# Prompt retention of a hybrid decoder layer: update and inner products as three passes of rounded parts

## The chip, the core and the metric

The kernel runs on one core of a Trainium2 chip. The metric is the device time of one execution in microseconds (us), lower is better. The engines are TensorE (PE for its matmuls, PEld for its weight loads), VectorE (DVE), ScalarE (ACT), GpSimd (POOL) and SyncE (SP), whose queue issues all the transfers here.

## The reference, cut to what matters

One decoder layer over 1024 prompt tokens and 64 sample tokens: projections, differential attention, retention, gated merge and a SwiGLU FFN, all in float32. The change touches the prompt's retention, which goes through 8 chunks of 128 tokens in each of 4 heads, with a state of 256x512:

```python
def ret_chunk(S, q, k, v, log_gamma):
    ...
    qk = jnp.einsum('bihd,bjhd->bhij', q, k) * decay[None]
    o = jnp.einsum('bhij,bjhe->bihe', qk, v)
    ...
    o = o + jnp.einsum('bihd,bhde->bihe', q * q_dec[None, :, :, None], S)
    ...
    S_new = jnp.exp(C * log_gamma)[None, :, None, None] * S + jnp.einsum('bjhd,bjhe->bhde', k * k_dec[None, :, :, None], v)
    return S_new, o
```

The sample tokens take one such step from a stored state; their part is computed in the same stretch of the kernel.

## The kernel before

The whole layer is one program for each engine, ordered by hand and tied by semaphores. Large matrix products run as three passes: weights and activations are held as a high part (rounded to fp32r) and a low part (the rest, rounded), and high x high, high x low and low x high are added up in PSUM. POOL makes both parts of each block of weights (`w_h`, L356, and `w_l`, L363).

The retention lies in a stage of its own. TensorE's row of work there is the gate projection: `ROWS = 32` rows of 24 slots, and a slot is three passes (L2046, `gate(n)` runs n slots). Between slots stand the pieces of 32 prompt chunks (`CHB`), one for every `BEAT = 21` slots, from slot `LAG = 96` on. Chunk c begins at slot `chunk_kg(c)`, called `at` below. At its start TensorE does `update(c, 0)` (L2079: half of the keys' contribution to the state) and `inner(c)` (L2085: masked scores times values), three slots later `rows_out` of the chunk before (L2101) and `across(c)` (L2092: queries times old state), at `at + 7` `update(c, 1)`, at `at + 10` the transposes of the next chunk's queries and keys (L2064), and at `at + 14` their product (L2071). All of these are fp32 matmuls. `sample_piece` puts the sample's work at fixed slots (L1968 to L2005).

The other engines keep in step through `Beside`: each walks its own list of slots up to a given one and then does a chunk's piece. ScalarE copies the transposes (L2201) and scales the keys by their decay (`k_dec`, L2209) at `at + 11`, and squares the output rows for their norm (L2220). DVE at `at + 4` multiplies the gate of the chunk before (L2351) and makes the new state's first half (L2343), at `at + 7` the norm (`dve_root`, Newton steps L2237 and L2239, then L2359), at `at + 9` the second half of the state, and at `at + 16` the masked score block of the next chunk (`between`, L2333). In rows 0 to 15 it also multiplies gates after each group of 8 slots (L2301). The sample's state updates on DVE are L2275. SP loads the next chunk's values (L1826) at `at + 10` and the queries and keys after that (L1820) at `at + 16`.

Buffers are views of large tiles: `acc` (here `acc1`, cut up by `fm_view`), `gain`, `edge` and `xs_flat`.

Of the kernel before, what the change touches and what calls it, by code (L numbers as in the profile page):

```python
# [34 lines left out]
D = 1024  # L35
# [157 lines left out]
def hybrid_layer(nc, x_prompt, x_sample, cache_k, cache_v, state_ret, page_table, norm_mix_g, w_in, b_gate,  # L193
# [54 lines left out]
    st.close()  # L248
    x_rows = acc1[:, :].rearrange("p (t d) -> p t d", d=D)
# [654 lines left out]
    def sp_vr_attention(sp):  # L904
# [68 lines left out]
        sp_load_inputs(sp, 0)  # L973
        store_half(2 * DH - 1)
# [708 lines left out]
    p_t = gain[:, 768:896]  # L1683
    np_t = gain[0:TS, 896:1024]
# [11 lines left out]
    k_dec = edge[:, 2944:3200]  # L1696
# [15 lines left out]
    kd_ready = sem("kd_ready")  # L1712
# [65 lines left out]
    def sp_load_inputs(sp, i):  # L1778

        sp.dma_start(n_decay, c_ret_new[i]).then_inc(n_loaded, 16)  # L1780
        sp.dma_start(n_qdec, c_ret_qdec[i]).then_inc(n_loaded, 16)
        sp.dma_start(nv_in, proj[TP:T, i * RV + VR:(i + 1) * RV + VR]).then_inc(n_loaded, 16)

    def sp_gates(sp):
# [47 lines left out]
        def load_own_keys(g):  # L1832

            if g == 0:
                sp.wait_ge(bank_full, G_FM)
            sp.wait_ge(own_ready, g + 1)
            for j in range(4):
                sp.dma_start(own_k[32 * j:32 * j + DS, :], own_rows(g, j, RK, KR)).then_inc(own_k_loaded, 16)
# [17 lines left out]
        def gate_steps():  # L1856

            for row in range(ROWS):
                g, r = divmod(row, 4)
                i = row // 8  # L1860
                for x in range(24):
# [7 lines left out]
                    if (r, x) == (1, 11) and g + 1 < 2 * RH:  # L1869
                        load_own_keys(g + 1)  # L1870
# [12 lines left out]
                    if (r, x) == (3, 1) and g + 1 < 2 * RH:  # L1883
                        load_own_values(g + 1)
# [73 lines left out]
    def pe_gates(pe):  # L1958
        def sample_piece(row, x):
# [30 lines left out]
            if (r, x) in UPDATES:  # L1990
# [6 lines left out]
                for q, bank in enumerate((BN, BA)):  # L1997
                    r0 = 32 * (2 * pair + q)
                    nc.tensor.matmul(psum[:, bank, :], own_k_dec[r0:r0 + DS, b * 128:(b + 1) * 128], own_v[r0:r0 + DS, :],  # L1999
                                     start=True, stop=True, tile_position=(r0, 0)).then_inc(nu_full, 1)  # L2000
# [132 lines left out]
    def act_gates(act):  # L2133
        def sample_piece(row, x):
# [3 lines left out]
            if (m, x) == (0, 14):  # L2138
                act.wait_ge(nt_full, i + 1)
                nc.scalar.copy(nqk_t, psum[:, BN, 0:2 * KT * TS].rearrange("p (k n) -> p k n", n=TS)).then_inc(nt_read, 1)  # L2140
            if (r, x) == (1, 2):
                act.wait_ge(own_k_loaded, 64 * (g + 1))
                act.wait_ge(rd_loaded[i % 2], 16 * (i // 2 + 1))
                act.wait_ge(nu_full, 8 * g)
                nc.scalar.activation(own_k_dec, own_k, ACT.Copy, scale=decay[i % 2][:, 132:133]).then_inc(own_ready, 1)
# [57 lines left out]
        def chunk_decay(c):  # L2203
# [5 lines left out]
            nc.scalar.activation(k_dec, rk_in, ACT.Copy, scale=decay[i % 2][:, 129:130]).then_inc(kd_ready, 1)  # L2209
# [3 lines left out]
        chunk_decay(0)  # L2213
        for c in range(CHB):
# [8 lines left out]
            if c + 1 < CHB:  # L2223
                chunk_t(c + 1)
                chunk_decay(c + 1)
        beside.to(math.inf)
# [17 lines left out]
    def dve_gates(dve):  # L2244
        def sample_piece(row, x):
# [14 lines left out]
            if (m, x) == (0, 20):  # L2260
                dve.wait_ge(nqk_full, i + 1)
                for h in range(2):
# [59 lines left out]
        dstep.done(nc.vector.memset(np_t, 0.0))  # L2322
# [4 lines left out]
        def between(c):  # L2327
# [5 lines left out]
            nc.vector.tensor_tensor(p_t, psum[:, BT, 0:128], decay[i % 2][:, 0:128], ALU.mult).then_inc(pt_ready, 1)  # L2333
# [27 lines left out]

        beside.to(LAG - 3)
        between(0)
        for c in range(CHB):
# [26 lines left out]
    tails = []  # L2391
    for kind, dt in (("f", F), ("r", R)):
        st = ExitStack()
        for half in ("high", "low"):
            sb(f"tail_{kind}_{half}", [128, KD * T], F, st)
        tails.append(sb(f"tail_{kind}", [128, KD * 128 + NT * D], dt, st))
        st.close()
    tail_f, tail_r = tails
# [791 lines left out]
```

## Time and profile before

| | us |
|---|---|
| median of 3 runs | 2775.54 |
| lowest, highest | 2775.37, 2775.61 |
| profiled execution, its own time | 2780.18 |
| its span | 2778.4 |
| TensorE matmuls busy | 2749.3 (99%) |
| DVE busy | 1280.8 (46%) |
| ScalarE busy | 720.0 (26%) |
| POOL busy | 862.8 (31%) |
| retention stage, chunks 0 to 31 | from 1068 to 1628 |

Times in rows of a timeline count from the first instruction of the profiled execution. Matmuls are pipelined and their busy times overlap, so what one costs is read from the distance of starts. A row of DVE that starts before the one ahead has ended is pipelined in the same way, by some 0.08 us.

### The profile page before, as it was taken

What the parts mean: (1) busy time and instruction counts of PE and PEld (TensorE: products, weight loads), DVE (VectorE), ACT (ScalarE), POOL (GpSimd) and SP (SyncE); (2) the same over time, 40 slices, a digit from 0 to 9 for tenths busy, and PEclk for the clock granted to TensorE, in tenths of its full rate; (3) what the DMA queues carried; (4) which work ended last, traced back from release to release, by engine and by line L of the source; (5) the groups of instructions that cost most, each with busy time, mean ns of one, the idle gap of its engine ahead of it and who ended that gap; (6) DMA issues with size and microseconds to landing.
All of it is one profiled execution on the core that took longest, in us unless ns stands there. A gap on an engine that the chain in (4) does not pass through costs nothing.

```text
span 2778.4 us, 41312 instructions
## 1 busy us (share of the span) xinstructions
PE 2749.3 (99%) x16146; PEld 2327.7 (84%) x16146; DVE 1280.8 (46%) x2468; ACT 720.0 (26%) x1518; POOL 862.8 (31%) x697
## 2 busy tenths in 40 slices
PE   8999999999999999999999999999999999999998
PEld 6888877777777778787777799999899999998886
DVE  6431355536555644454444432343375555543224
ACT  5111122225555532222111221011232222221011
POOL 2433422202211222221122233535023444455240
PEclk9999999999999999999999999999999999999999
DMA  4323356553333234456555454243122222245221
GB/s 149 119 92 133 106 197 205 201 168 123 97 121 126 82 126 165 156 186 193 183 168 180 154 196 139 103 148 137 66 89 70 71 79 86 71 148 173 84 60 64
DMA packets 277776, 362.11 MB, mean 130 GB/s; under 512 B 28514, under 2 KB 172514, under 8 KB 277602
## 3 DMA queue, kind: packets, MB, share of 16 engines
q1 hardware_dynamic: 277602, 359.74, 39.0%
q8 instruction: 116, 1.90, 0.3%
q14 instruction: 58, 0.48, 0.1%
HBM read 257.24 MB, written 111.35 MB: 133 GB/s over the span
## 4 chain that ended last, share of the span: by engine, by line
PE 95%; DVE 2%; ACT 1%; issue 1%; DMA 1%; SPq 0%; ACTq 0%; DVEq 0%
PE psum L530 22%; PE psum L1318 14%; PE psum L2677 14%; PE psum L2046 13%; PE psum L555 10%; PE psum L1011 3%; PE psum L1037 2%; PE psum L2659 2%; PE psum L2079 2%; PE psum L2092 2%; PE psum L1999 1%; PE psum L2701 1%; PE psum L1432 1%; PE psum L1027 1%; PE psum L2085 1%; PE psum L989 1%
## 5 line engine op out<-in xcount | busy, mean ns | idle before, releaser
L356 POOL TENSOR_TENSOR w_h<-stage,ones 128x512 fp32r<-128x512 f32 x268 | 303.8, 1161 | 1336.3 <-PE psum L2046 414.1
L363 POOL TENSOR_TENSOR w_l<-stage,w_h 128x512 fp32r<-128x512 f32 x268 | 355.8, 1355 | 123.4 <-DVE acc L1159 118.7
L530 PE MATMUL psum<-w_h,xt_h 128*128 128x512 f32 x864 | 344.4, 399 | 2.9 <-POOL w_l L377 2.0
L530 PE MATMUL psum<-w_h,xt_l 128*128 128x512 f32 x864 | 342.6, 396 | 0.0
L530 PE MATMUL psum<-w_l,xt_h 128*128 128x512 f32 x864 | 342.5, 396 | 0.0
L2046 PE MATMUL psum<-xt_h,w_h 128*128 128x384 f32 x744 | 288.8, 388 | 0.1
L2046 PE MATMUL psum<-xt_h,w_l 128*128 128x384 f32 x744 | 244.6, 329 | 0.0
L2046 PE MATMUL psum<-xt_l,w_h 128*128 128x384 f32 x744 | 244.6, 329 | 0.0
L408 POOL TENSOR_TENSOR w_l<-stage,w_h 128x512 fp32r<-128x512 f32 x106 | 139.3, 1314 | 268.8 <-ACT w_h L2771 268.7
L1318 PE MATMUL psum<-w_h,xt_h 128*128 128x512 f32 x512 | 218.1, 426 | 0.0
L1318 PE MATMUL psum<-w_l,xt_h 128*128 128x512 f32 x512 | 202.1, 395 | 0.0
L1318 PE MATMUL psum<-w_h,xt_l 128*128 128x512 f32 x512 | 201.7, 394 | 0.0
L530 PEld LDWEIGHTS psum<-w_h,xt_h 128*128 128x128 f32 x864 | 163.2, 189 | 44.4 <-issue 3.1
L530 PEld LDWEIGHTS psum<-w_l,xt_h 128*128 128x128 f32 x864 | 163.1, 189 | 39.4
L530 PEld LDWEIGHTS psum<-w_h,xt_l 128*128 128x128 f32 x864 | 163.2, 189 | 38.3
L2046 PEld LDWEIGHTS psum<-xt_h,w_h 128*128 128x128 f32 x744 | 140.6, 189 | 51.9 <-issue 50.5
L2677 PE MATMUL psum<-tail_r,w_h 128*128 128x272 f32 x648 | 172.2, 288 | 0.0
L2046 PEld LDWEIGHTS psum<-xt_l,w_h 128*128 128x128 f32 x744 | 140.7, 189 | 19.9 <-issue 19.9
L2907 DVE TENSOR_TENSOR acc<-acc,psum 128x512 f32<-128x512 f32 (+1 forms) x72 | 49.4, 687 | 209.3 <-PE psum L530 189.7
L2046 PEld LDWEIGHTS psum<-xt_h,w_l 128*128 128x128 f32 x744 | 140.1, 188 | 0.0
L555 PE MATMUL psum<-xt_h,w_h 128*128 128x384 f32 (+1 forms) x576 | 126.5, 328 | 0.0
L555 PE MATMUL psum<-xt_h,w_l 128*128 128x384 f32 (+1 forms) x576 | 126.5, 327 | 0.0
(300 smaller groups left out, 5584.3 us busy)
## 6 DMA issues: line engine op xcount, KB each, us to landing
stage<-in_w_in_dram SPq DMA_DIRECT2D x88, 512.0 KB, 5.7
proj<-edge SPq DMA_DIRECT2D x112, 256.0 KB, 2.0
out_dram<-acc SPq DMA_DIRECT2D x44, 512.0 KB, 3.5
stage<-in_w_gu_dram SPq DMA_DIRECT2D x88, 256.0 KB, 3.9
acc<-proj SPq DMA_DIRECT2D x82, 256.0 KB, 3.0
gates<-edge SPq DMA_DIRECT2D x32, 544.0 KB, 4.3
acc<-in_cache_k_dram SPq DMA_DIRECT2D x32, 512.0 KB, 5.7
acc<-in_cache_v_dram SPq DMA_DIRECT2D x32, 512.0 KB, 4.5
```

Of the source, the lines that this page charges most:

```text
L356: last = nc.gpsimd.tensor_tensor(w_h[s][:, a:b, :], src, one.unsqueeze(1).to_broadcast([128, b - a, WN]), ALU.mult)
L363: last = nc.gpsimd.tensor_tensor(w_l[s][:, a:b, :], stage[h][:, a - lo:b - lo, :], w_h[s][:, a:b, :].bitcast(F), ALU.subtract)
L408: nc.gpsimd.tensor_tensor(op_l(o), op_source(n, name), op_h(o).bitcast(F), ALU.subtract).then_inc(op_split, 1)
L530: last = nc.tensor.matmul(psum[:, bank, :], x, w[s][:, k, :], start=k == 0 and n == 0, stop=k == nk - 1 and n == len(passes) - 1)
L555: ins = nc.tensor.matmul(psum[:, g(3 * j + c)[1], 0:width], w[s][:, k, m * 128:(m + 1) * 128], x[:, k, a:a + width], start=k == 0 and n == ...
L1011: nc.tensor.matmul(psum[:, SB_ + 2 * c + a // 512, 0:width], q[r, qb % 4 * 128:(qb % 4 + 1) * 128], k_t[(2 * h + a // 512) % 3][r, 0:width ...
L1037: last = nc.tensor.matmul(psum[:, TB, 0:DV], mix_t[:, b * 128:(b + 1) * 128], v_in[(2 * h + b // 4) % 3][:, b % 4, :], start=b == 0, stop= ...
L1318: last = nc.tensor.matmul(psum[:, VB + u % 2, :], x, wt[s][:, k, :], start=k == 0 and n == 0, stop=k == KD - 1 and n == len(passes) - 1)
L2046: last = nc.tensor.matmul(psum[:, BG + q % 2, 0:width], wt[s][:, k, m * 128:(m + 1) * 128], x[:, k, a:a + width], start=k == 0 and n == 0, ...
L2079: nc.tensor.matmul(psum[:, BU, :], k_dec[:, k * 128:(k + 1) * 128], rv_in, start=True, stop=True).then_inc(upd_full, 1)
L2092: last = nc.tensor.matmul(psum[:, BO, :], qk_t[:, k, :], state[:, k, :], start=False, stop=k == KT - 1)
L2677: last = nc.tensor.matmul(psum[:, 2 * (no % 4) + c, 0:HC], w(o)[:, k, :], x_piece(x, k, low)[:, at], start=k == 0 and i == 0, stop=k == 3 ...
```

## The change

`update` and `inner` no longer multiply in fp32 but in three passes of fp32r parts. For that ScalarE writes the decayed keys rounded (`k_dec_high`) and, new at `at + 15`, the values rounded (`rv_high`). DVE writes the rest of the keys at `at + 13` (`k_dec_low`), makes the masked score block twice (`p_t` in fp32, `p_high` rounded) and subtracts (`p_low`), and at `at + 17` writes the rest of the values over the loaded ones (`rv_low`). One semaphore, `kv_split`, counts the four steps of a chunk; both updates wait for all four. The rounded parts lie in `tail_r`, an fp32r view of memory that `acc` and `xs_flat` cover.

To make room, the sample's values (`nv_in`) share `nr_rows` and load at slot 9 in place of 3 of a head's last row, its transposed queries and keys and its score block move into `gain`, with a memset for each head, and the own keys are scaled in place and loaded at slot 1 of a group's row 3 in place of slot 11 of row 1.

```diff
+    rv_in_at = fm_at[0]
     rv_in = fm_view(128, RV)
...
-    nv_in = fm_view(TS, RV)
     nr_rows = fm_view(128, RV)
+    nv_in = nr_rows[0:TS, :]
+    rv_at = fm_at[0]
+    fm_view(128, RV)
...
-    nqk_t = xs_flat[:, 0:256].rearrange("p (k n) -> p k n", n=TS)
+    p_high, p_low, p_t = tail_r[:, 0:128], tail_r[:, 128:256], xs_flat[:, 128:256]
+    rv_high, rv_low = (tail_r[:, KD * 128 + a:KD * 128 + a + RV] for a in (rv_at, rv_in_at))
     q_own = xs_flat[:, 256:512].rearrange("p (k b r) -> p k b r", k=KT, r=16)
-    own_k, own_k_dec = (xs_flat[:, 512 + RK * s:512 + RK * (s + 1)] for s in range(2))
+    k_dec_high, k_dec_low = (tail_r[:, 512 + RK * s:512 + RK * (s + 1)] for s in range(2))
...
         def load_chunk(c):
             if c >= 1:
                 sp.wait_ge(rt_full, c)
-                sp.wait_ge(kd_ready, c)
+                sp.wait_ge(kv_split, 4 * c - 2)
...
-                    if (r, x) == (1, 11) and g + 1 < 2 * RH:
-                        load_own_keys(g + 1)
...
                     if (r, x) == (3, 1) and g + 1 < 2 * RH:
+                        load_own_keys(g + 1)
                         load_own_values(g + 1)
...
+                    if row % 8 == 7 and x == 9 and i + 1 < RH:
+                        sp_load_own_rows(sp, i + 1)
...
         def update(c, k):
-            pe.wait_ge(kd_ready, c + 1)
-            pe.wait_ge(rv_loaded, 16 * (c + 1))
+            pe.wait_ge(kv_split, 4 * (c + 1))
             pe.wait_ge(state_ready, 2 * c + k)
-            nc.tensor.matmul(psum[:, BU, :], k_dec[:, k * 128:(k + 1) * 128], rv_in, start=True,
-                             stop=True).then_inc(upd_full, 1)
+            for n, (keys, values) in enumerate(((k_dec_high, rv_high), (k_dec_low, rv_high), (k_dec_high, rv_low))):
+                last = nc.tensor.matmul(psum[:, BU, :], keys[:, k * 128:(k + 1) * 128], values, start=n == 0, stop=n == 2)
+            last.then_inc(upd_full, 1)
 
         def inner(c):
             pe.wait_ge(pt_ready, c + 1)
             pe.wait_ge(rnorm_ready, c)
-            last = nc.tensor.matmul(psum[:, BO, :], p_t, rv_in, start=True, stop=c % NC == 0)
+            for n, (weights, values) in enumerate(((p_high, rv_high), (p_low, rv_high), (p_high, rv_low))):
+                last = nc.tensor.matmul(psum[:, BO, :], weights, values, start=n == 0, stop=c % NC == 0 and n == 2)
...
+        def values_high(c):
+
+            act.wait_ge(rv_loaded, 16 * (c + 1))
+            act.wait_ge(kv_split, 4 * c + 2)
+            nc.scalar.copy(rv_high, rv_in).then_inc(kv_split, 1)
...
+                dstep.done(nc.vector.memset(np_t, 0.0))
+                dstep.wait(dve)
...
-            nc.vector.tensor_tensor(p_t, psum[:, BT, 0:128], decay[i % 2][:, 0:128], ALU.mult).then_inc(pt_ready, 1)
+            dstep.done(nc.vector.tensor_tensor(p_t, psum[:, BT, 0:128], decay[i % 2][:, 0:128], ALU.mult))
+            dstep.done(nc.vector.tensor_tensor(p_high, psum[:, BT, 0:128], decay[i % 2][:, 0:128], ALU.mult))
+            dstep.wait(dve)
+            nc.vector.tensor_tensor(p_low, p_t, p_high.bitcast(F), ALU.subtract).then_inc(pt_ready, 1)
+
+        def keys_low(c):
+
+            i = c // NC
+            dve.wait_ge(kv_split, 4 * c + 1)
+            nc.vector.scalar_tensor_tensor(k_dec_low, rk_in, decay[i % 2][:, 129:130], k_dec_high.bitcast(F), ALU.mult,
+                                           ALU.subtract).then_inc(kv_split, 1)
+
+        def values_low(c):
+
+            dve.wait_ge(kv_split, 4 * c + 3)
+            nc.vector.tensor_tensor(rv_low, rv_in, rv_high.bitcast(F), ALU.subtract).then_inc(kv_split, 1)
...
-            beside.to(at + 16)
             if c + 1 < CHB:
+                beside.to(at + 13)
+                keys_low(c + 1)
+                beside.to(at + 16)
                 between(c + 1)
+                beside.to(at + 17)
+                values_low(c + 1)
```

DVE at the end of chunk 5, from the norm's last operation to the gate product behind the score block of chunk 6 (`waits` names the semaphores; lines are each kernel's own). Before:

```order
L2359 TENSOR_SCALAR acc<-psum,rope_diff,o_rstd 128x512 [waits dve_step]
L2301 TENSOR_TENSOR edge<-edge 128x384 [waits sg_ready]
L2255 TENSOR_TENSOR xs_flat<-xs_flat,gain 128x4x8 [waits nr_full,n_loaded,nt_read]
L2255 TENSOR_TENSOR xs_flat<-xs_flat,gain 128x4x8 x3
L2343 SCALAR_TENSOR_TENSOR acc<-acc,rope_diff,psum 128x512 [waits ro_full,upd_full]
L2263 TENSOR_TENSOR gain<-psum,edge 64x4x8 [waits nqk_full]
L2263 TENSOR_TENSOR gain<-psum,edge 64x4x8
L2301 TENSOR_TENSOR edge<-edge 128x320 [waits sg_ready]
L2333 TENSOR_TENSOR gain<-psum,rope_diff 128x128 [waits gate_mul,ro_full,qk_full,rd_loaded0]
L2301 TENSOR_TENSOR edge<-edge 128x384 [waits sg_ready]
```

The same place after the change, from the second half of the state on:

```order
L2392 SCALAR_TENSOR_TENSOR acc<-acc,rope_diff,psum 128x512 [waits ro_full,upd_full]
L2295 MEMSET gain 64x128 [waits nq_ready,nqk_full]
L2298 TENSOR_TENSOR gain<-psum,edge 64x4x8 [waits dve_step]
L2298 TENSOR_TENSOR gain<-psum,edge 64x4x8
L2376 SCALAR_TENSOR_TENSOR tail_r<-acc,rope_diff,tail_r 128x256 [waits kv_split]
L2336 TENSOR_TENSOR edge<-edge 128x320 [waits sg_ready]
L2367 TENSOR_TENSOR xs_flat<-psum,rope_diff 128x128 [waits gate_mul,ro_full,qk_full,rd_loaded0]
L2368 TENSOR_TENSOR tail_r<-psum,rope_diff 128x128
L2370 TENSOR_TENSOR tail_r<-xs_flat,tail_r 128x128 [waits dve_step]
L2382 TENSOR_TENSOR tail_r<-acc,tail_r 128x512 [waits kv_split]
L2336 TENSOR_TENSOR edge<-edge 128x384 [waits sg_ready]
```

The keys' low part (L2376) comes in ahead of the gate product, and three operations stand where the score block (L2333, now L2367) was the last: its second copy, its low part, and the values' low part (L2382).

TensorE at the start of chunk 6. Before:

```order
L2046 MATMUL psum<-xt_h,w_l 128x384
L2079 MATMUL psum<-acc,edge 128x512 [waits state_ready,rv_loaded,kd_ready]
L2085 MATMUL psum<-acc,gain 128x512 [waits rnorm_ready,pt_ready]
L2046 MATMUL psum<-xt_h,w_h 128x384
L2046 MATMUL psum<-xt_l,w_h 128x384
```

After:

```order
L2065 MATMUL psum<-xt_h,w_l 128x384
L2098 MATMUL psum<-tail_r 128x512 [waits state_ready,kv_split]
L2098 MATMUL psum<-tail_r 128x512 x2
L2105 MATMUL psum<-tail_r 128x512 [waits rnorm_ready,pt_ready]
L2105 MATMUL psum<-tail_r 128x512 x2
L2065 MATMUL psum<-xt_h,w_h 128x384
L2065 MATMUL psum<-xt_l,w_h 128x384
```

Two fp32 matmuls become six passes at the same place; the update's wait is now for `kv_split`, whose last step is DVE's L2382.

## Rows read from the trace of the kernel before

**Rows 1.** The page: busy time of TensorE, and the granted clock in 40 slices.
```profile
PE 2749.3 (99%) x16146; PEld 2327.7 (84%) x16146; DVE 1280.8 (46%) x2468; ACT 720.0 (26%) x1518; POOL 862.8 (31%) x697
...
PEclk9999999999999999999999999999999999999999
```

**Rows 2.** Waits, 1060 to 1628 us: total, times, longest.
```profile
POOL w_h L356 <- PE psum L2046: 414.1, 7, 64.4
...
PE psum L1999 <- DVE acc L2275: 0.9, 1, 0.9
```

**Rows 3.** Groups of instructions, 1060 to 1628 us: count, busy us, mean ns.
```profile
L2079 PE MATMUL psum<-acc,edge 128*128 128x512 f32 x128 | 65.3, 592 | 0.0
...
L2085 PE MATMUL psum<-acc,gain 128*128 128x512 f32 x64 | 32.7, 592 | 0.0
```

**Rows 4.** Timeline of TensorE, start of chunk 15: start, us, line.
```profile
1330.82 1.02 PE L2079 MATMUL psum<-acc,edge 128*128 128x512 f32 x2
1331.68 1.02 PE L2085 MATMUL psum<-acc,gain 128*128 128x512 f32 x2
...
1332.72 0.34 PE L2046 MATMUL psum<-xt_l,w_h 128*128 128x384 f32 x1
```

**Rows 5.** Timeline of TensorE in an earlier projection, 26 passes, first and last.
```profile
300.04 0.40 PE L530 MATMUL psum<-w_h,xt_h 128*128 128x512 f32 x1
...
305.88 0.39 PE L530 MATMUL psum<-w_h,xt_l 128*128 128x512 f32 x1
```

**Rows 6.** Single lines: duration in ns, min/median/max; the last is a group.
```profile
L2301 DVE TENSOR_TENSOR edge<-edge x48: 474/558/1326, 1018.4 to 1311.5; 128x384 f32<-128x384 f32 x32, 128x320 f32<-128x320 f32 x16
...
L2524 DVE TENSOR_TENSOR xt_l<-acc,xt_h x8: 1285/1294/2249, 1621.9 to 1643.2; 128x1088 fp32r<-128x1088 f32 x8
...
L2343 DVE SCALAR_TENSOR_TENSOR acc<-acc,rope_diff,psum x56: 736/744/750, 1087.5 to 1629.9; 128x512 f32<-128x512 f32 x56
...
L2201 ACT COPY acc<-psum 128x512 f32<-128x512 f32 x32 | 18.8, 587 | 67.1 <-PE psum L2064 66.8 <-ACT edge L2165 0.3
```

**Rows 7.** Timeline, DVE's score block and TensorE's update: chunks 1, 5, 6, 10, 24.
```profile
1080.62 0.28 DVE L2333 TENSOR_TENSOR gain<-psum,rope_diff 128x128 f32<-128x128 f32 x1
...
1082.06 1.02 PE L2079 MATMUL psum<-acc,edge 128*128 128x512 f32 x2
...
1150.70 0.29 DVE L2333 TENSOR_TENSOR gain<-psum,rope_diff 128x128 f32<-128x128 f32 x1 [0.24 <-DVE edge L2301]
...
1153.92 1.02 PE L2079 MATMUL psum<-acc,edge 128*128 128x512 f32 x2
...
1171.08 1.02 PE L2079 MATMUL psum<-acc,edge 128*128 128x512 f32 x2
...
1171.34 0.29 DVE L2333 TENSOR_TENSOR gain<-psum,rope_diff 128x128 f32<-128x128 f32 x1 [0.24 <-DVE edge L2301]
...
1240.85 0.28 DVE L2333 TENSOR_TENSOR gain<-psum,rope_diff 128x128 f32<-128x128 f32 x1
...
1241.98 1.02 PE L2079 MATMUL psum<-acc,edge 128*128 128x512 f32 x2
...
1490.39 0.28 DVE L2333 TENSOR_TENSOR gain<-psum,rope_diff 128x128 f32<-128x128 f32 x1
...
1490.47 1.02 PE L2079 MATMUL psum<-acc,edge 128*128 128x512 f32 x2
```

**Rows 8.** A Newton step's durations, two rows of a timeline, and POOL's groups, 1060 to 1628.
```profile
L2239 DVE SCALAR_TENSOR_TENSOR o_rstd<-o_newton,o_rstd x108: 159/159/1218, 1071.6 to 1628.7; 128x1 f32<-128x1 f32 x108
...
1162.81 5.00 POOL L363 TENSOR_TENSOR w_l<-stage,w_h 128x512 fp32r<-128x512 f32 x4
...
1164.13 1.21 DVE L2239 SCALAR_TENSOR_TENSOR o_rstd<-o_newton,o_rstd 128x1 f32<-128x1 f32 x1
...
L363 POOL TENSOR_TENSOR w_l<-stage,w_h 128x512 fp32r<-128x512 f32 x56 | 70.8, 1295 | 1.1
...
L356 POOL TENSOR_TENSOR w_h<-stage,ones 128x512 fp32r<-128x512 f32 x56 | 58.5, 1076 | 414.1 <-PE psum L2046 414.1
```

**Rows 9.** The load of a chunk's values, L1826, from issue to landing.
```profile
DMA to landing us min/median/max: 2.6/2.8/6.2
```

More of the change, by code:

```diff
@@ L248, in hybrid_layer @@
     st.close()
+    tails = []
+    for kind, dt in (("f", F), ("r", R)):
+        st = ExitStack()
+        for half in ("high", "low"):
+            sb(f"tail_{kind}_{half}", [128, KD * T], F, st)
+        tails.append(sb(f"tail_{kind}", [128, KD * 128 + NT * D], dt, st))
+        st.close()
+    tail_f, tail_r = tails
     x_rows = acc1[:, :].rearrange("p (t d) -> p t d", d=D)
@@ L973, in sp_vr_attention @@
         sp_load_inputs(sp, 0)
+        sp_load_own_rows(sp, 0)
         store_half(2 * DH - 1)
@@ L1682, in hybrid_layer @@
     nr_gate = gain[:, 512:768].rearrange("p (b n) -> p b n", b=VT)
-    p_t = gain[:, 768:896]
-    np_t = gain[0:TS, 896:1024]
+    nqk_t = gain[:, 768:1024].rearrange("p (k n) -> p k n", n=TS)
+    np_t = gain[0:TS, 768:896]
     n_qdec = gain[:, 1024:1088]
@@ L1711, in hybrid_layer @@
     rt_read = sem("rt_read")
-    kd_ready = sem("kd_ready")
+    kv_split = sem("kv_split")
     qk_full = sem("qk_full")
@@ L1781, in sp_load_inputs, with sp_load_own_rows @@
         sp.dma_start(n_qdec, c_ret_qdec[i]).then_inc(n_loaded, 16)
+    def sp_load_own_rows(sp, i):
+        sp.wait_ge(nrr_full, i)
         sp.dma_start(nv_in, proj[TP:T, i * RV + VR:(i + 1) * RV + VR]).then_inc(n_loaded, 16)
@@ L1836, in load_own_keys @@
             sp.wait_ge(own_ready, g + 1)
+            sp.wait_ge(nu_full, 8 * g)
             for j in range(4):
@@ L1998, in sample_piece @@
                     r0 = 32 * (2 * pair + q)
-                    nc.tensor.matmul(psum[:, bank, :], own_k_dec[r0:r0 + DS, b * 128:(b + 1) * 128], own_v[r0:r0 + DS, :],
+                    nc.tensor.matmul(psum[:, bank, :], own_k[r0:r0 + DS, b * 128:(b + 1) * 128], own_v[r0:r0 + DS, :],
                                      start=True, stop=True, tile_position=(r0, 0)).then_inc(nu_full, 1)
@@ L2139, in sample_piece @@
                 act.wait_ge(nt_full, i + 1)
+                act.wait_ge(nr_full, 2 * i)
+                if i == 0:
+                    act.wait_ge(a_stored[1], 16 * DH)
                 nc.scalar.copy(nqk_t, psum[:, BN, 0:2 * KT * TS].rearrange("p (k n) -> p k n", n=TS)).then_inc(nt_read, 1)
@@ L2143, in sample_piece @@
                 act.wait_ge(rd_loaded[i % 2], 16 * (i // 2 + 1))
-                act.wait_ge(nu_full, 8 * g)
-                nc.scalar.activation(own_k_dec, own_k, ACT.Copy, scale=decay[i % 2][:, 132:133]).then_inc(own_ready, 1)
+                nc.scalar.activation(own_k, own_k, ACT.Copy, scale=decay[i % 2][:, 132:133]).then_inc(own_ready, 1)
             if (m, x) == (1, 9):
@@ L2208, in chunk_decay @@
             act.wait_ge(upd_full, 2 * c)
-            nc.scalar.activation(k_dec, rk_in, ACT.Copy, scale=decay[i % 2][:, 129:130]).then_inc(kd_ready, 1)
+            nc.scalar.activation(k_dec_high, rk_in, ACT.Copy, scale=decay[i % 2][:, 129:130]).then_inc(kv_split, 1)
+        def values_high(c):
+            act.wait_ge(rv_loaded, 16 * (c + 1))
+            act.wait_ge(kv_split, 4 * c + 2)
+            nc.scalar.copy(rv_high, rv_in).then_inc(kv_split, 1)
         beside.to(LAG - 7)
@@ L2213, in act_gates @@
         chunk_decay(0)
+        beside.to(LAG - 3)
+        values_high(0)
         for c in range(CHB):
@@ L2225, in act_gates @@
                 chunk_decay(c + 1)
+                beside.to(at + 15)
+                values_high(c + 1)
         beside.to(math.inf)
@@ L2261, in sample_piece @@
                 dve.wait_ge(nqk_full, i + 1)
+                dve.wait_ge(nq_ready, i + 1)
+                dstep.done(nc.vector.memset(np_t, 0.0))
+                dstep.wait(dve)
                 for h in range(2):
@@ L2321, in dve_gates @@
         dstep.done(nc.vector.memset(q_own, 0.0))
-        dstep.done(nc.vector.memset(np_t, 0.0))
         nc.vector.memset(own_k, 0.0).then_inc(own_ready, 1)
@@ L2360, in normalise @@
                                     ALU.mult).then_inc(rnorm_ready, 1)
+        beside.to(LAG - 5)
+        keys_low(0)
         beside.to(LAG - 3)
         between(0)
+        beside.to(LAG - 2)
+        values_low(0)
         for c in range(CHB):
@@ L2390, in hybrid_layer @@
     h_keep = nc.dram_tensor("h_keep", [T, D], F).ap()
[L2391 to L2398, printed above, removed]
     READ_BY = {"A11": "c11", "S2": "u2", "A12": "c11", "S3": "u3", "S1": "u4", "A22": "c21", "S4": "c12"}
```

2 lines of the change are left out of this document (1 added, 1 removed).

## The prediction

> **What bounds the kernel now.** I read the page first: TensorE is busy 99% of the span, at 2.4 GHz (nine tenths or more of full speed granted in every slice), and the profiled execution took 2780.2 us with a span of 2778.4, against a median of 2775.54 [rows 1]. The list of waits, cut to the retention stage (1060 to 1628 us), then shows whom TensorE waits for there: only DVE's sample update, 0.9 us of 568 [rows 2]. So whatever makes TensorE's row of work shorter moves the end one for one, unless another engine is now late. POOL and ScalarE wait for TensorE in that stage and not the other way round; POOL's split of the next weights waits 414 us for it.
>
> **What the change takes off TensorE.** An update or an inner product was one fp32 instruction in the program, and shows as two records of 128x512, busy 592 ns each but overlapping [rows 3]. The start times tell the real price: update and inner product of chunk 15 (chunks are counted from 0) start at 1330.82 and the second gate matmul behind them at 1332.72; one gate matmul's pitch of 0.176 lies between, so two products take 1.72 us, 0.86 each [rows 4]. A pass of rounded parts of the same shape is in the trace in the earlier projections: 25 starts from 300.04 to 305.88, 0.2336 us each [rows 5]. Three are 0.70. The gain is 0.159 us for a product; there are 32 chunks with two updates and one inner product, 96 products: **15.3 us**. Bounds: the passes are the same kind of instruction with the same shape, so 0.2336 is close; 0.225 and 0.245 would give 17.8 and 12.0 us. The weight loads of these passes hide as those of the projections do, whose pitch contains them. Transposes, products of queries and keys, and the part of the old state stay fp32 and cost what they did.
>
> **What it adds.** Each chunk gets one more ScalarE operation (the values rounded, 128x512; the nearest row is the copy at 0.587 us) and four more on DVE: low part of the keys (128x256), a second masked score block and its low part (128x128), low part of the values (128x512). Update(c, 0) now waits for the last of these, and inner(c) for the score parts. Behind the waiting update stand all gate matmuls on TensorE, so a wait there moves the end.
>
> Durations: two-input DVE operations from SBUF take 0.558 us at 384 columns and 1.29 at 1088 [rows 6], 1.04 ns for a column, so 0.69 at 512 and 0.29 at 128; the scalar-tensor-tensor at 256 is L2343's 0.744 less 256 columns, 0.48. Operations that don't depend on each other start some 0.08 before the one ahead ends. From the end of the old score block (L2333) to the first pass of the update it is then 0.21 (second block) + 0.32 (low part, which waits for it) + 0.61 (values) + 0.25 (semaphore and the weight load that a waiting matmul can't hide; 0.1 to 0.3) = 1.39 us. TensorE comes 0.16 sooner, since update(c-1, 1) is shorter: 1.55. Where DVE is behind and works without a pause, the keys' low part pushes too: **1.95 us**.
>
> The slack against this is the start of L2079 less the end of L2333. In 25 of the 32 chunks it is 2.1 to 5.5 us, more than is needed outside POOL's stretches but in chunk 9. The short ones and one long one [rows 7]: chunk 10 has 1241.98 - 1241.13 = 0.85, and DVE is behind, so it waits 1.95 - 0.85 = 1.1. In the same way chunk 1 has 1.16, but its values' low part also stands behind a gate product (0.48 more): 1.3; chunk 24 has -0.2: 2.1; chunk 6 has -0.55, with a pause of 0.24 that takes some up: 2.3. Chunks 0, 14 and 15 (slack 1.2, 0.9, 0.8) give 0.2, 0.35 and 1.1; chunk 9, again behind a gate product, 0.3. Sum: **8.8 us**.
>
> Chunks 6, 10 and 15 are short because DVE got there late, and the rows say why [rows 8]: while POOL splits weights (seven stretches of 18 to 19 us in the stage), the small Newton steps of DVE, which read two SBUF operands, take 0.96 to 1.32 us in place of 0.16 and 0.22, each until one POOL instruction (1.08 or 1.30) has ended; operations with a PSUM operand keep their time. Three of the four new DVE operations have two SBUF operands, and so have this price: a wait to the end of POOL's running instruction, 0 to 1.3 us, for each. The Trainium skill, SBUF — State Buffer, section "Who interferes with whom", says the same: a DVE instruction with two SBUF inputs and a GpSimd instruction that reads SBUF exclude each other for the whole instruction; this rule speaks against the change, for without it the sum of waits would end at 8.8. Laying the new operations between the rows of DVE and POOL, each held to the end of the POOL instruction in which it would start, adds 0.8 in chunk 1, 1.7 in chunk 5 (which had 2.9 of slack), 0.9 in chunk 10, 1.0 in chunk 14, 0.8 in chunk 19 and 0.5 in chunk 24: **5.7 us**, 4 to 9 with POOL's stretches moved by up to 4 us against the chunks. (Chunk 5 is the long one among the rows.)
>
> What costs nothing, with its cover: the rounding on ScalarE (value load issued 1 us after the update, landing in 2.8 us, 6.2 at most [rows 9]; the copy then ends 2.2 us or more before the next update, and ScalarE waits for TensorE around it; if a landing takes 6 us in each chunk, 2 us are lost); the own keys' load moved from row 1 to row 3 of a group, past the store and load of the states on SP's queue, with its 1.5 us of issue and still over 20 us ahead of its scaling; the sample rows' values loaded eight slots later, over 10 us ahead of their use; a memset of 64x128 for each head (0.15 us on DVE, four times, two of them in chunks that are short: 0.3); the chunk load on SP that waits for the keys' low part, a whole chunk ahead.
>
> **Sum.** -15.3 + 8.8 + 5.7 + 0.3 for the memsets = -0.5 us. On the profiled execution 2780.2 becomes 2779.7; on the median, which lies 4.6 below it, 2775.0. A measurement here can tell about 0.2%, 5.6 us, from no change, so this is no change.
>
> **Rivals.**
> - *The waits stay at 8.8*: the port between DVE and POOL costs the new operations little, because they slip in between POOL instructions. For it: the gate products at 384 columns that meet POOL's stretches mostly take under 0.7 and only at worst 1.33 [rows 6]. Then -15.3 + 8.8 + 0.3 = -6.2: 2769.3.
> - *Hardly a wait*: DVE's lateness in chunks 6, 15 and 24 is chance of this execution's phase, and shorter TensorE work moves POOL's stretches away from the Newton steps. Then some 3 us of waits, -12: 2763. Against it: the stretches are released by TensorE itself, in the same rows of the gates, so the phase repeats.
> - *Slower*: the new operations lose their turn against POOL more than once. The place is the end of chunks 1, 5, 10, 14, 19 and 24; one more POOL instruction (1.2 us) in each is +7.2, the sum +6.7, 2782.2. It decides from a second lost turn a chunk on. Chunk by chunk POOL's instructions follow each other without a gap, which speaks for it; the Newton steps, which each get in after one, against it.
> - *The passes aren't cheap*: a pass at 0.29 us or more would eat the whole gain, and at the fp32 record's 0.43 the change would cost 41 us. The rows of the projections leave this 2 in 100.
>
> **How the numbers follow.** The forecast, with its waits of 10 to 19 us, 2771 to 2780: 0.56. Waits near 8.8: 0.18. Hardly a wait: 0.11. Lost turns: 0.13. Dear passes: 0.02. Faster by over 0.2% (below 2770.0) takes the hardly-a-wait case and most of the 8.8 case: 0.27; slower (above 2781.1) most of the lost turns and the dear passes: 0.14; within it 0.59. The forecast's own range is 2771 to 2780; the range of 8 in 10 takes in 2769 and some of the lost turns: 2766 to 2781.5.
>
> **What would show it.** Right: three passes of update and inner product starting 0.234 apart; TensorE waiting for DVE's values' low part, 8 to 11 times in 32, 1 to 3 us at a time, 12 to 17 us in all, at the ends of chunks 1, 5, 6, 10, 14, 15, 19 and 24; the new two-input DVE operations at 0.3 to 0.7 us outside POOL's stretches and up to 1.3 longer in them. Wrong: waits on the ScalarE rounding or on the value load; waits spread over all chunks; a sum of waits under 5 us; passes at another pitch.

## The result, and the profile after

The changed kernel takes **2784.65 us** (median of 8 runs, 2781.2 to 2787.5); the kernel before, beside it, 2775.74 (8 runs). (Of all runs below, one of the kernel with fp32 products and waits and one of the kernel before beside it took some 13 ms; they are left out.) The ratio is 1.0029, interval 1.0019 to 1.0040: slower by 8 us, 5 to 11. The forecast was 2775.0, no change, in a range of 2766 to 2781.5. The measured time lies beyond the range, on the side that had 14 in 100.

The profiled execution took 2784.83 us with a span of 2782.6. From the page, busy time, and under it the waits of TensorE in the whole span (us in total, times, longest):

```profile
PE 2739.6 (98%) x16242; PEld 2346.9 (84%) x16242; DVE 1339.6 (48%) x2599; ACT 739.0 (27%) x1550; POOL 867.5 (31%) x697
```

```profile
PE psum L2098 <- DVE tail_r L2382: 13.1, 7, 3.9
...
PE psum L2018 <- DVE acc L2310: 1.7, 2, 1.1
```

TensorE is busy 10 us less than before [rows 1], DVE 59 us more. A wait that [rows 2] didn't have is now the largest of TensorE: seven updates (L2098) wait for the low part of the values (L2382), 13.1 us in all. So far this is the forecast. What it didn't have is in the granted clock, in stretches of 10 us of the changed kernel behind three of these waits, and behind the longest of the others (columns: length, TensorE busy with its count, granted clock, share and GB/s of DMA):

```profile
1083.50:1093.50 10.00, 9.61 (x40) 0.83 0.20 71
1175.50:1185.50 10.00, 9.75 (x37) 0.66 0.08 31
1250.00:1260.00 10.00, 9.75 (x42) 0.83 0.16 46
1322.50:1332.50 10.00, 9.78 (x49) 1.00 0.10 28
...
1498.50:1508.50 10.00, 9.75 (x54) 1.00 0.20 70
```

A mean of 0.83 over 10 us is 3.4 us at 1.2 GHz in place of 2.4, and 0.66 is 6.8 us. The half of it is lost: 1.7, 3.4 and 1.7 us, 6.8 us that the kernel before did not lose at these places. This is one profiled execution, but the others agree in their mean granted clock: 0.995 or 0.996 in all eight of the changed kernel, 0.998 or 0.999 in all 66 of the kernel before that ran beside the experiments. The difference of the means, 0.003, is some 8 us of such a span (an estimate; 0.001 is 2.8 us). In chunk 1 the six passes of update and inner product follow the wait (timeline of TensorE; in brackets the 3.88 us of idle time ahead). They take 2.5 us, up to the gate matmul at 1086.40; six at 0.234 are 1.4:

```profile
1083.89 1.44 PE L2098 MATMUL psum<-tail_r 128*128 128x512 f32 x3 [3.88 <-DVE tail_r L2382]
1085.12 1.48 PE L2105 MATMUL psum<-tail_r 128*128 128x512 f32 x3
...
1086.40 0.47 PE L2065 MATMUL psum<-xt_h,w_h 128*128 128x320 f32 x1
```

The account of the stage goes from the first to the last matmul of the gate projection. L2046 started first at 1008.4 and last at 1617.1 us before; its counterpart after is

```profile
L2065 PE MATMUL psum<-xt_h,w_h x744: 302/337/741, 1006.6 to 1622.2; 128*128 128x384 f32 x124, 128*128 128x320 f32 x62
```

That is 608.7 us before and 615.6 after, +6.9. The passes bring -15.3; TensorE's pauses grew by 13.2 (from 1.7 to 15.0 us, summed over the timelines) and, since a pause is counted from the modelled end of a matmul 0.34 long that the next could have followed after 0.18, by some 1.1 more (seven pauses more than before); the clock took 6.8. The sum is +5.8, and 1.1 is left over. (By whole executions the two profiled ones are 4.7 us apart, since that of before lay 4.4 us over its median; 1.7 of it is a fall of the clock at 28 us, ahead of the stage.)

### The profile page after: what moved, and what is told of

It is laid out like the page before. It is cut to its first block, busy times and chain, and to the rows that moved or that the text cites. A ratio compares the mean times of both kernels' runs of the same rounds, so it can differ in the third digit from the quotient of the medians.

```text
span 2782.6 us, 41714 instructions
## 1 busy us (share of the span) xinstructions
PE 2739.6 (98%) x16242; PEld 2346.9 (84%) x16242; DVE 1339.6 (48%) x2599; ACT 739.0 (27%) x1550; POOL 867.5 (31%) x697
## 4 chain that ended last, share of the span: by engine, by line
PE 93%; DVE 4%; ACT 1%; issue 1%; DMA 1%; SPq 0%; DVEq 0%; ACTq 0%
PE psum L538 22%; PE psum L1327 14%; PE psum L2726 14%; PE psum L2065 12%; PE psum L563 10%; PE psum L1020 3%; PE psum L1046 2%; PE psum L2708 2%; PE psum L2112 2%; PE psum L2098 2%; PE psum L2018 1%; PE psum L2750 1%; PE psum L1441 1%; PE psum L1036 1%; PE psum L2105 1%
## 5 line engine op out<-in xcount | busy, mean ns | idle before, releaser
L2065 PE MATMUL psum<-xt_h,w_h 128*128 128x384 f32 x744 | 266.0, 358 | 0.1
L563 PE MATMUL psum<-xt_l,w_h 128*128 128x384 f32 (+1 forms) x576 | 126.5, 327 | 0.0
```

The costliest lines, as they stand in the source:

```text
L563: ins = nc.tensor.matmul(psum[:, g(3 * j + c)[1], 0:width], w[s][:, k, m * 128:(m + 1) * 128], x[:, k, a:a + width], start=k == 0 and n == ...
L2065: last = nc.tensor.matmul(psum[:, BG + q % 2, 0:width], wt[s][:, k, m * 128:(m + 1) * 128], x[:, k, a:a + width], start=k == 0 and n == 0, ...
```

## The experiments

Twelve kernels ran, each beside the kernel before on the same chip. In each diff the lines are those of the changed kernel unless said otherwise.

### The passes alone

```diff
-            pe.wait_ge(kv_split, 4 * (c + 1))
+            pe.wait_ge(kv_split, 2 * (c + 1))
...
-            for n, (keys, values) in enumerate(((k_dec_high, rv_high), (k_dec_low, rv_high), (k_dec_high, rv_low))):
+            for n, (keys, values) in enumerate(((k_dec_high, rv_high), (k_dec_high, rv_high), (k_dec_high, rv_high))):
...
-                keys_low(c + 1)
-                values_low(c + 1)
```

> Three passes as in the change, but all of the high parts; the low parts of keys, scores and values are left out (three DVE operations and the second score block less a chunk), the moves of the sample's buffers stay. Theory (the passes bring 15.3 us, and what was lost is waits for DVE's values and TensorE's clock after them): no waits of the update, no fall of the clock in the stage but the one at its end, 2760 to 2761 us, ratio 0.9945. Rival (the passes cost more than 0.2336 us in this place, or the moved buffers cost): 2766 us or more, without waits.

The diff is cut: the inner product takes its high parts three times in the same way, and the second score block, its low part and ScalarE's wait for the keys' low part are gone too.

Measured: 2761.27 us, ratio 0.9939 (0.9924 to 0.9954). TensorE waits for none of the parts. The groups of the passes, with nothing idle before them:

```profile
L2098 PE MATMUL psum<-tail_r 128*128 128x512 f32 x192 | 54.8, 394 | 0.0
L2105 PE MATMUL psum<-tail_r 128*128 128x512 f32 x96 | 27.3, 393 | 0.0
```

By the ratio the gain is 16.9 us (13 to 21). In the trace the gate's first matmuls start from 1005.5 to 1599.2, 593.7 us in place of 608.7: 15.0 us less, with the same two short waits for the sample and the same fall of the clock at the stage's end as before. That is the forecast's 15.3, and the moved buffers of the sample cost nothing that shows. What the changed kernel loses comes with the low parts and the waits for them.

### The waits without the gain

```diff
-            for n, (keys, values) in enumerate(((k_dec_high, rv_high), (k_dec_low, rv_high), (k_dec_high, rv_low))):
-                last = nc.tensor.matmul(psum[:, BU, :], keys[:, k * 128:(k + 1) * 128], values, start=n == 0, stop=n == 2)
-            last.then_inc(upd_full, 1)
+            nc.tensor.matmul(psum[:, BU, :], k_dec_low.bitcast(F)[:, k * 128:(k + 1) * 128], rv_low.bitcast(F), start=True,
+                             stop=True).then_inc(upd_full, 1)
```

> The changed kernel with one fp32 product in the place of each three passes, on the low parts' tiles (the values come out other): all the splitting and its waits, without the gain. Theory (gain 15.3 us, waits 13, clock 7): the changed kernel's time plus 15 us, less up to 2 for waits that shorten since TensorE comes later: 2798 to 2801 us, ratio 1.008 to 1.009. Rival (the passes brought much less than 15 us): 2790 or less.

The inner product is changed in the same way.

Measured: 2795.01 us, ratio 1.0065 (1.0047 to 1.0084), 3 us under the expected range. The trace says why: waits of 11.9 us in place of 13.1, and only two falls of the clock of 3.4 us at the waits, in place of 13.6 us in three places, 3.4 us less lost. 15.3 less these two is 10.7. The fall at the stage's end is missing in this profile too, 1.7 us more, which makes 9.0; the two profiled executions are 8.7 us apart, the medians 10.4.

```profile
PE psum L2097 <- DVE tail_r L2380: 11.9, 6, 3.9
```

### Does the wait bring the clock down?

A ladder of waits in the kernel **before**, which has no fp32r product in the chunks:

```diff
+        AGAIN = {7: 18, 12: 22, 16: 24, 21: 29, 26: 32}
...
+            for _ in range(AGAIN.get(c, 0)):
+                dstep.done(nc.vector.tensor_tensor(p_t, psum[:, BT, 0:128], decay[i % 2][:, 0:128], ALU.mult))
+                dstep.wait(dve)
             nc.vector.tensor_tensor(p_t, psum[:, BT, 0:128], decay[i % 2][:, 0:128], ALU.mult).then_inc(pt_ready, 1)
```

> The kernel before, fp32 products; DVE repeats the masked score block 18, 22, 24, 29 and 32 times in chunks 7, 12, 16, 21 and 26, so that the inner product of each waits some 0.9, 2, 3, 4 and 5 us. Theory (a wait of about 2 us or more makes the granted clock fall from 2.4 to 1.2 GHz for 3.4 us or twice that just after it): no fall after the first, one at least after each of the last three, 1.7 us lost for each 3.4. Rival (the falls in the changed kernel came from its fp32r passes or from POOL's stretches, and only happened to stand behind waits): none here.

The waits came out as meant (timeline of TensorE, in brackets the idle time ahead):

```profile
1191.53 0.70 PE L2085 MATMUL psum<-acc,gain 128*128 128x512 f32 x1 [0.82 <-DVE gain L2338]
...
1282.29 1.12 PE L2085 MATMUL psum<-acc,gain 128*128 128x512 f32 x2 [1.95 <-DVE gain L2338]
...
1356.82 1.22 PE L2085 MATMUL psum<-acc,gain 128*128 128x512 f32 x1 [3.04 <-DVE gain L2338]
...
1451.17 1.76 PE L2085 MATMUL psum<-acc,gain 128*128 128x512 f32 x2 [4.05 <-DVE gain L2338]
...
1547.93 1.22 PE L2085 MATMUL psum<-acc,gain 128*128 128x512 f32 x1 [5.20 <-DVE gain L2338]
```

and the granted clock in the 10 us from each (the number behind the count in brackets):

```profile
1191.00:1201.00 10.00, 9.47 (x40) 1.00 0.68 239
1282.00:1292.00 10.00, 9.71 (x50) 1.00 0.47 159
1356.00:1366.00 10.00, 9.18 (x32) 0.66 0.51 189
1451.00:1461.00 10.00, 9.83 (x36) 0.83 0.10 29
1547.00:1557.00 10.00, 9.07 (x31) 0.66 0.40 138
```

There is no fall at the waits of 0.8 and 1.95 us, and one at each of the longer three, 6.8, 3.4 and 6.8 us long. Two of them begin 0.9 us before the wait is over, one 0.4 us after it. So a wait alone does it, with neither the new passes nor their operands, and without POOL: in this trace POOL splits no weights from 1330 to 1399, 1417 to 1484 and 1503 to 1575 us, where the three lie. The kernel took 2801.06 us in its one run: 15 us of waits and 8.5 us of clock over the kernel before.

The other way round: in the changed kernel DVE is as late as it was, but TensorE works through three of the waits.

```diff
+        FILL = {1: 15, 6: 12, 10: 7}
...
+            if c in FILL:
+                pe.wait_ge(rnorm_ready, c)
+                for n in range(FILL[c]):
+                    nc.tensor.matmul(psum[:, BO, :], xt_h1[:, 0, 0:128], xt_h1[:, 0, 0:512], start=True, stop=True)
             update(c, 0)
```

> The changed kernel; in chunks 1, 6 and 10 TensorE fills the time of the update's wait with 15, 12 and 7 extra fp32r passes of 128x512, into the bank that the inner product overwrites. Theory (clock): the waits for DVE stay, the filled time costs nothing since it was waited, and the clock doesn't fall there: 6 to 7 us less than the changed kernel, 2778 us, ratio 1.0006. Rival (the fall has nothing to do with the idle time): falls as before, 2785 or more.

Measured: 2780.24 us, ratio 1.0010 (1.0001 to 1.0019), against 1.0029 of the changed kernel: 5.3 us less by the ratios, 4.4 by the medians, where 6.5 were expected. The clock stays up in all three places:

```profile
1084.00:1094.00 10.00, 9.48 (x48) 1.00 0.23 82
1175.00:1185.00 10.00, 9.75 (x50) 1.00 0.17 66
1246.00:1256.00 10.00, 9.79 (x51) 1.00 0.22 58
```

At most 0.5 us of each of the three waits is left idle. Beside the changed kernel the starts tell what the three falls cost by themselves: update(1, 0) starts 1.60 us later in the filled kernel's trace and the first update of chunk 2 only 0.05; that of chunk 6 starts 0.03 later and that of chunk 7 3.21 earlier; that of chunk 10 3.21 and that of chunk 11 4.76 earlier. That is 1.55, 3.24 and 1.55 us, 6.3 in all, for the same work behind the same end of each wait. So TensorE's idle time brings these falls, and they cost about half their length. The Trainium skill, TensorE: Matmul & The Clock Gate, section "What's actually happening", says that activity holds the clock up and idleness throttles it; the two runs agree.

### Who makes DVE late?

POOL's splits of the stage's weights are cut to 8 of 512 columns (the blocks' other columns stay stale, so the gates come out other); `width` is handed on to the two POOL operations:

```diff
-        split_loop(16, 4)
+        split_loop(16, 4, width=8)
```

> The changed kernel; POOL's splits of the eight weight blocks made in this stage (two of them the merge's) take 8 of 512 columns, so the rest of those blocks is left stale. Theory (DVE is late because its operations on two SBUF operands wait for POOL's instructions): Newton steps at 0.16 and 0.22 us throughout, the waits of the update fall from 13 us to under 1 us, no fall of the clock but the stage's last: 2762 us, ratio 0.995. Rival (the four new DVE operations are too much in themselves): chunks 1, 6 and 24 still wait about 2 us each, 2768 or more.

Measured: 2762.51 us, ratio 0.9948 (0.9933 to 0.9963). TensorE waits for no low part, and the Newton steps, up to 1328 ns in the changed kernel, stay at their own time throughout:

```profile
L2269 DVE SCALAR_TENSOR_TENSOR o_newton<-o_rstd,o_var x108: 218/219/233, 1069.9 to 1611.2; 128x1 f32<-128x1 f32 x108
```

All seven waits are POOL's doing. The forecast had read DVE's lateness in chunks 6, 10 and 15 so; those of chunks 1 and 24, for which it gave no cause, are POOL's too. The four new operations fit into the slack when nobody holds them up. This run takes away both parts of the forecast's sum, the lateness that was there (8.8 us) and the new operations' own waits for POOL (5.7), and cannot tell them apart.

### The loop over ScalarE

ScalarE's rounding of the values waits for the count of the keys' low part, though it reads nothing of it. In the changed kernel, chunk 6, on ScalarE:

```profile
1172.24 0.62 ACT L2237 CAST tail_r<-acc 128x512 fp32r<-128x512 f32 x1 [4.33 <-DVE tail_r L2376]
1172.77 0.43 ACT L2185 ACTIVATE edge<-psum 128x320 f32<-128x320 f32 x1
1173.10 0.42 ACT L2187 COPY edge<-psum 128x320 f32<-128x320 f32 x1
```

and on DVE, whose next operation needs that copy, ahead of the score block and the values:

```profile
1171.69 0.47 DVE L2376 SCALAR_TENSOR_TENSOR tail_r<-acc,rope_diff,tail_r 128x256 fp32r<-128x256 f32 x1
1173.55 0.49 DVE L2336 TENSOR_TENSOR edge<-edge 128x320 f32<-128x320 f32 x1 [1.39 <-ACT edge L2187]
1174.28 0.29 DVE L2367 TENSOR_TENSOR xs_flat<-psum,rope_diff 128x128 f32<-128x128 f32 x1 [0.24 <-DVE edge L2336]
...
1175.01 0.68 DVE L2382 TENSOR_TENSOR tail_r<-acc,tail_r 128x512 fp32r<-128x512 f32 x1
```

A semaphore of its own for the values takes the loop apart (the waits of the updates, of DVE and of SP count accordingly):

```diff
-            act.wait_ge(kv_split, 4 * c + 2)
-            nc.scalar.copy(rv_high, rv_in).then_inc(kv_split, 1)
+            act.wait_ge(rv_split, 2 * c)
+            nc.scalar.copy(rv_high, rv_in).then_inc(rv_split, 1)
```

> The changed kernel; the values' two steps count on a semaphore of their own, so that ScalarE's rounding no longer waits for the keys' low part from DVE. Theory (part of the waits is a loop: DVE late, so ScalarE's rounding late, so the gate unit behind it late, so DVE's gate product and the values' low part late): the pause of DVE before its gate product in chunk 6 (1.39 us) goes, the waits in chunks 1 and 6 shrink by 1 to 2 us each, the sum of waits by 3 to 5 us, one or two of the clock's three falls go: 2777 us, ratio 1.0005. Rival (the waits are DVE's own work and POOL's alone): within 1 us of the changed kernel's 2784.65.

Measured: 2778.12 us, ratio 1.0002 (0.9993 to 1.0011), 7.5 us less than the changed kernel by the ratios. The waits of chunks 1 and 6 are 2.78 and 1.60 us in place of 3.88 and 3.06, the others as they were:

```profile
1080.79 1.49 PE L2100 MATMUL psum<-tail_r 128*128 128x512 f32 x3 [2.78 <-issue]
...
1171.16 0.93 PE L2100 MATMUL psum<-tail_r 128*128 128x512 f32 x3 [1.60 <-issue]
```

That is 2.2 us of waits less in the stage. Of the clock's falls at the waits, that of chunk 1 is 3.4 us as before, those of chunks 6 and 10 are gone, and one of 3.4 us is new in chunk 24, after 2.02 us: 6.8 us at 1.2 GHz in place of 13.6, 3.4 us less lost. Together 5.6 of the 7.5 us are seen in this profile; the clock's part is the larger.

### Later, and both

```diff
-            update(c, 0)
-            inner(c)
             gate(3)
+            update(c, 0)
+            inner(c)
             if c:
                 rows_out(c - 1)
```

> The changed kernel with update(c, 0) and inner(c) three gate slots later, right ahead of rows_out(c-1), so that DVE has 1.6 us more. Theory: each wait of the update is 1.6 us shorter: chunks 1, 6, 10, 24 keep 2.3, 1.5, 0.2, 0.4 and the others none, some 4.5 us in all, at most one fall of the clock: 2768 us, ratio 0.997. Rival (the engines behind, which wait for the update and the inner product, get late in their turn): 2775 or more.

> Both: the values' own semaphore and the update and inner product three slots later. Theory: waits of 1.2 us in chunk 1, 0.3 to 0.4 in chunks 10 and 24 and no others, no fall of the clock after them: 2762 to 2763 us, ratio 0.9952, faster than both kernels. Rival as for the kernel with the later update alone: 2770 or more.

Measured: 2773.20 us, ratio 0.9986 (0.9977 to 0.9995), and with the own semaphore 2773.36, ratio 0.9985 (0.9976 to 0.9994). Both are faster than before and than the changed kernel, but 5 and 11 us short of what was expected, and with the later update the own semaphore adds nothing. In the kernel with the later update alone the waits of chunks 6, 14, 15 and 19 went and that of chunk 24 is 0.41 us, but that of chunk 1 is 3.81 us (3.88 in the changed kernel) and that of chunk 10 has grown from 1.82 to 2.68, each with a fall of 3.4 us. With the own semaphore they are 3.85 and 2.72. Chunk 10's, in the kernel with the later update alone:

```profile
1244.92 1.47 PE L2098 MATMUL psum<-tail_r 128*128 128x512 f32 x3 [2.68 <-DVE tail_r L2382]
```

The rival's mechanism shows here, though its 2775 was not reached with the later update alone (its 2770 was with both). With the inner product the norm of the same chunk begins later too, and so does all that DVE does behind it. In chunk 0 five of the six Newton steps are held up by POOL, and the last is over at 1076.94, 1.0 us later than in the changed kernel (1075.93); 1.0 of the 1.6 us that the update gained is gone by then. The values' low part of chunk 1 is over 1.2 us later than in the changed kernel.

```profile
1070.98 1.23 DVE L2271 SCALAR_TENSOR_TENSOR o_rstd<-o_newton,o_rstd 128x1 f32<-128x1 f32 x1
1072.24 1.21 DVE L2269 SCALAR_TENSOR_TENSOR o_newton<-o_rstd,o_var 128x1 f32<-128x1 f32 x1
...
1075.98 0.96 DVE L2271 SCALAR_TENSOR_TENSOR o_rstd<-o_newton,o_rstd 128x1 f32<-128x1 f32 x1
```

### Newton steps that POOL can't hold up

The same arithmetic with both factors as scalars of a partition, so that one SBUF tensor is read and not two:

```diff
-            dstep.done(nc.vector.scalar_tensor_tensor(z, y, v, y, ALU.mult, ALU.mult))
+            dstep.done(nc.vector.tensor_scalar(z, y, v, y, ALU.mult, ALU.mult))
...
-            dstep.done(nc.vector.scalar_tensor_tensor(y, z, c, y, ALU.add, ALU.mult))
+            dstep.done(nc.vector.tensor_scalar(y, z, c, y, ALU.add, ALU.mult))
```

> The changed kernel with the two Newton operations of DVE written as tensor-scalar operations (both factors as per-partition scalars, same arithmetic), so that they read one SBUF tensor and not two. Theory (POOL makes DVE late through the Newton steps, and that is what the update waits for in chunks 1, 6, 10 and 15): steps at about 0.15 us in POOL's stretches too, DVE 5 to 6 us earlier there, no wait in chunks 6, 10, 15, 1 us or less in chunk 1, some 5 us of waits left (chunks 14, 19, 24), no or one fall: 2767 to 2770 us, ratio 0.997. Rival (a tensor-scalar waits for POOL as well, or the new operations' own waits for POOL carry the loss): 2780 or more.

> The same with the values' own semaphore. Theory: the loop over ScalarE only lengthened waits of 2 us and more, which are gone; so within 2 us of the kernel with the Newton steps alone, 2766 to 2769 us. Rival (the loop costs in every chunk): 5 us or more less.

> Newton steps, own semaphore, and update and inner product three slots later. Theory: no wait of the update longer than 0.5 us, no fall of the clock but the stage's last: 2761 to 2763 us, the passes' whole 15 us, ratio 0.9945 to 0.995. Rival (the later update makes DVE's chain late in its turn, as in chunks 1 and 10 of the kernel with both): 2767 or more.

> The kernel before with the tensor-scalar Newton steps. Theory: TensorE waits for DVE 0.9 us in the stage, so nothing is to be had: within 1.5 us of before, ratio 1.000. Rival (DVE's lateness cost something there already): 3 us or more less.

The steps take 0.27 and 0.21 us, POOL or not, where 0.15 had been expected:

```profile
L2269 DVE TENSOR_SCALAR o_newton<-o_rstd,o_var x108: 272/273/277, 1068.8 to 1626.1; 128x1 f32<-128x1 f32 x108
```

Alone in the changed kernel they give 2775.70 us, ratio 0.9997 (0.9988 to 1.0007): 9 us less than the changed kernel, but 6 over what was expected. The updates still waited 8.0 us in all, where some 5 had been expected: 1.47 in chunk 1, 1.74 in chunk 24 and, against the expectation, 2.81 in chunk 6. There DVE came to the sample's four small products (two SBUF operands each) while POOL ran, and they took 3.86 us. ScalarE's rounding of the values waited 4.08 us, until the keys' low part was done, and DVE's gate product behind it 1.39: the loop again. The clock fell for 10.2 us, from 0.9 us before the wait was over:

```profile
1162.01 3.86 DVE L2287 TENSOR_TENSOR xs_flat<-gain 128x32 f32<-128x32 f32 x4
```

```profile
1170.97 1.65 PE L2098 MATMUL psum<-tail_r 128*128 128x512 f32 x3 [2.81 <-DVE tail_r L2382]
```

```profile
1170.00:1180.00 10.00, 9.03 (x26) 0.51 0.14 56
```

With the own semaphore too: 2771.70, ratio 0.9983 (0.9973 to 0.9992), 4 us less than with the Newton steps alone. The expected range of 2766 to 2769 was missed by 3 us, and the loop is worth more than I gave it, though less than the rival's 5 us: chunk 6's wait is 0.19 us now, and this profile, of the fastest of the ten runs, shows no fall of the clock at all in the stage.

With the update three slots later as well: **2762.02 us, ratio 0.9950 (0.9933 to 0.9966)**, as expected. TensorE waits for the low part once, 0.2 us (the group of the update's passes; idle time ahead of it in the last columns):

```profile
L2100 PE MATMUL psum<-tail_r 128*128 128x512 f32 x192 | 54.9, 394 | 0.2 <-issue 0.2
```

This is the passes' gain in full within the intervals (the passes alone had 0.9939, 0.9924 to 0.9954), and the fastest kernel of this study that computes the layer in full. The Newton steps alone in the kernel before: 2777.87, ratio 1.0004 (0.9994 to 1.0014), no change, as expected: they are worth something only where somebody waits for DVE.

## Why the prediction was wrong

**The gain was right.** Forecast 15.3 us; with the passes alone the stage is 15.0 us shorter in the trace, and the kernel takes 2761.3 us.

**The sum of the waits was right, its parts less so.** Forecast 14.5 us (8.8 and 5.7), found 13.2 us of pauses more than before, 14.3 with the modelled ends. By chunks, forecast and found: 0: 0.2, none; 1: 2.1, 3.9; 5: 1.7, none; 6: 2.3, 3.1; 9: 0.3, none; 10: 2.0, 1.8; 14: 1.4, 1.0; 15: 1.1, 0.6; 19: 0.8, 0.7; 24: 2.6, 2.0. The step on POOL held: the values' low part took 677 ns at least and 1774 at most, the scores' 291 to 872, each longer only in POOL's stretches. All seven chunks that waited stood among the ten of the sum; eight to eleven waits had been named. One term was too large everywhere: the 0.25 us for the semaphore and a weight load had no row behind it, and in all seven waits the update's first pass starts 0.05 us after L2382 ends. So part of the agreement of the sums is luck.

**The step that failed was the price of a microsecond of wait.** The sum took a wait of TensorE as lost once, at its length, and had no term for the clock. Three of the waits cost more than their length, because the granted clock fell to 1.2 GHz at them: 6.8 us in the profile (6.3 by the filled waits), most of the 8.5 us between the forecast's -0.5 and the measured +8.0. The ladder and the filled waits show it. The remaining 2 us or so are not placed one by one.

The prediction read the granted clock only as a row of nines, and no rival had it. It took nine tenths or more of full speed in every slice for 2.4 GHz throughout; but a slice of [rows 1] is 69 us long, and a nine can hide a fall of 3.4 us. The trace of the kernel before has two, each with a pause of TensorE just ahead. The second lies in the stage, behind the one wait that [rows 2] shows (first TensorE's timeline, then a stretch of 10 us with its granted clock):

```profile
1592.99 1.13 PE L1999 MATMUL psum<-acc,xs_flat 8*128 8x512 f32 x4 [0.92 <-DVE acc L2275]
```

```profile
1593.00:1603.00 10.00, 10.00 (x42) 0.83 0.60 220
```

The first stands at 28 us, 3.4 us long, at a pause of 1.89 us. So the rows before already had pauses that cost 1.7 us more than their length, and the forecast's waits of 1 to 3 us needed a term for that.

**The step on ScalarE failed.** "What costs nothing" gave the rounding of the values 2.2 us of cover against the load, but not against its wait for DVE's count. That wait closed a loop (DVE late, rounding late, gate unit late, DVE's gate product late), which made the waits of chunks 1 and 6 1.1 and 1.5 us longer, enough to matter for the clock. Taking the loop apart gave 7.5 us in the changed kernel, waits and falls together, 4 us with the new Newton steps and nothing with the later update.

**The rival "the waits stay at 8.8"** is against the trace: it had the new operations slip in between POOL's, and they took up to 1.1 us longer in its stretches. How the waits divide into older lateness and the new operations' own stays open. The Newton steps alone brought the updates' waits from 13.1 to 8.0 us; without POOL nothing waits at all. **The rival "hardly a wait"** fell with the waits of chunks 6, 15 and 24, which stayed in their places.

**The rival "slower"** gave the right side for the wrong reason: the new operations are longer than outside POOL's stretches by 1.1 us at most, less than one POOL instruction of 1.3.

## What to carry to other kernels

A wait on the engine that sets the time can cost more than its length: where TensorE pauses for a microsecond or two or more, look at the granted clock in the 10 us around its end (a row of nines in 40 slices does not show it), and put the fall into the price before making a busy row shorter. When work moves to an engine with time to spare, its average share (46% here) says nothing; read the latency in the stretches in which another engine holds it up, and cure what is small and late already (here the Newton steps) before adding to it. A counter shared by two engines orders more than the data needs; give each chain its own.

## What the runs showed of the hardware

- TensorE's granted clock, from one profile of each kernel. At the updates and at the ladder's inner products, no pause of 0.5 to 1.8 us came with a fall; of those from 1.8 to 2.1 us some did (1.82 in the changed kernel, 2.02 with the own semaphore) and some did not (1.88, 1.95, 1.97, 1.98); each from 2.7 to 5.2 us did, thirteen of thirteen. These falls began between 0.9 us before the pause's end and 1.2 us after it. Elsewhere the length does not sort them so: at the stage's last sample update a fall followed pauses of 0.9 to 1.7 us in eight of the fourteen profiles (0.92 in the kernel before, 1.06 in the changed one), and none followed 1.07 and 1.73 us in others; near 28 us a pause of 1.89 us had one and pauses of 1.86 and 2.35 us in other profiles had none.
- A tensor-scalar operation of DVE with two per-partition scalars (the Newton step L2269) takes 0.27 us on one column, and 0.27 in POOL's stretches as well, where the scalar-tensor-tensor took 0.22 alone and up to 1.33.
- Operations of DVE that POOL holds up can wait one by one: four products of 128x32, 0.18 us each alone, took 3.86 us together.
